# Transposed projections of two mixers as 512-column products with values and rests side by side, and their halves added on the way out of PSUM

## What is computed

```python
# first mixer
q, k, v = jnp.split(x @ w_qkv, 3, axis=-1)
...
# second mixer
u = h @ w_in
cuts = [CONV_WIDTH, 2 * CONV_WIDTH, 3 * CONV_WIDTH, 3 * CONV_WIDTH + LRU_WIDTH]
a_b, a_c, a_x, r_gate, r_x = jnp.split(u, cuts, axis=-1)
y_a = a_b * causal_depthwise_conv(a_c * a_x, conv_a_w)
xr = causal_depthwise_conv(r_x, conv_b_w) + conv_b_b
y_b = jax.nn.gelu(r_gate) * rg_lru(xr, rg_a_w, rg_a_b, rg_x_w, rg_x_b, rg_lambda)
y = jnp.concatenate([y_a, y_b], axis=-1) @ w_out
```

## Time and profile before

| | |
|---|---|
| median of 3 executions | 890.99 us |
| the profiled execution's own time | 891.4 us |
| its span | 889.3 us |
| instructions | 13261 |
| TensorE busy (matmul) | 880.2 us, 99% |
| VectorE busy | 694.1 us, 78% |
| ScalarE busy | 501.6 us, 56% |
| GpSimd busy | 29.0 us, 3% |

### The profile page before, as it was taken

One profiled execution on the slowest core, in us unless ns is written; L12 is line 12 of the kernel. 1 busy time (PEld: TensorE's weight loads), 2 busy tenths in 40 slices (PEclk: granted clock), 3 DMA queues, 4 the chain that ended last, 5 costly groups with the idle time before them and its releaser, 6 DMA issues.

```text
span 889.3 us, 13261 instructions
## 1 busy us (share of the span) xinstructions
PE 880.2 (99%) x4833; PEld 747.9 (84%) x4833; DVE 694.1 (78%) x735; ACT 501.6 (56%) x673; POOL 29.0 (3%) x52
## 2 busy tenths in 40 slices
...
DMA packets 117091, 208.04 MB, mean 234 GB/s; under 512 B 7236, under 2 KB 81068, under 8 KB 111928
## 3 DMA queue, kind: packets, MB, share of 16 engines
...
...
q0 software_dynamic: 192, 0.05, 0.0%
...
## 4 chain that ended last, share of the span: by engine, by line
PE 93%; DVE 4%; DMA 2%; issue 1%; ACT 1%; SPq 0%; DVEq 0%; ACTq 0%
PE ub L1937 11%; PE tp L1937 10%; PE acc L1837 7%; PE acc L1838 7%; PE acc L1840 7%; PE ub L1939 5%; PE acc L1800 5%; PE tp L1939 5%; PE acc L1802 5%; PE acc L1801 5%; PE tp L1957 4%; PE acc L1957 3%; PE acc L1923 3%; PE acc L1925 3%; PE acc L1924 3%; PE ub L2183 1%
## 5 line engine op out<-in xcount | busy, mean ns | idle before, releaser
L1157 DVE TENSOR_TENSOR w_lo<-w_raw,w_hi 128x1024 fp32r<-128x1024 f32 x283 | 341.8, 1222 | 105.1 <-ACT w_hi L728 104.7
L728 ACT ACTIVATE w_hi<-w_raw 128x1024 fp32r<-128x1024 f32 x283 | 296.8, 1057 | 211.9 <-PE acc L1840 49.8
L1937 PE MATMUL tp<-aT,w_hi 128*128 128x512 f32 x432 | 135.9, 396 | 0.0
L1937 PE MATMUL ub<-aT,w_hi 128*128 128x512 f32 x432 | 135.4, 395 | 0.0
L1837 PE MATMUL acc<-w_hi,hT_hi 128*128 128x512 f32 x284 | 110.8, 390 | 0.8 <-DVE w_lo L1157 0.8
L1838 PE MATMUL acc<-w_lo,hT_hi 128*128 128x512 f32 x284 | 110.6, 389 | 0.0
L1840 PE MATMUL acc<-w_hi,hT_lo 128*128 128x512 f32 x272 | 105.8, 389 | 0.0
L1939 PEld LDWEIGHTS tp<-aT,w_lo 128*128 128x128 f32 x432 | 81.2, 188 | 19.2
L1939 PEld LDWEIGHTS ub<-aT,w_lo 128*128 128x128 f32 x432 | 81.1, 188 | 18.9
L1939 PE MATMUL tp<-aT,w_lo 128*128 128x256 f32 x432 | 84.9, 278 | 0.0
L1939 PE MATMUL ub<-aT,w_lo 128*128 128x256 f32 x432 | 84.9, 278 | 0.0
...
## 6 DMA issues: line engine op xcount, KB each, us to landing
...
```

What stands on the lines that cost most here:

```text
L728: act.activation(rounded_part(v), w_raw[:, v % SLOTS, :], ACT.Copy).then_inc(hi_done, 1)
L1157: dve.tensor_tensor(rest_part(v), w_raw[:, v % SLOTS, :], rounded_part(v).bitcast(F32), ALU.subtract).then_inc(lo_done, 1)
L1937: pe.matmul(banks[f], rounded_part(v)[:, c[f]], aT[:, :, b, :], start=b == 0, stop=False)
```

## The change

U2 to U7 of the first mixer and U2 to U9 of the second become wide units. A unit now fills a pair of banks by itself: columns 0 to 255 of each bank get rounded weight by rounded values and weight's rest by rounded values, columns 256 to 511 rounded weight by the activation's rests. New steps F n get unit n out: ScalarE copies the second halves to SBUF (`rest_half`, semaphore `t_rest`), VectorE adds the first halves (`sum_halves`, semaphore `t_sum`). Units take turns on two pairs of banks (`wide_banks`), so a unit waits for the sum of the unit two before it; U8 of the second mixer has `ub`, U9 `tp`. The gelu of E1 is then done in SBUF. W1 moves from after H10 to after H8. The old step F0 of VectorE is now called N0. Cut to its core, the diff:

```diff
-ATT_STEPS = steps("""L1 U0 H2 L2 U1 H3 E0 L3 U2 H4 T0 L4 U3 H5 L5 E1 X0 G0 G1 U4 H6 L6 Y0 U5 H7 E2 S0 L7 G2 G3 G4 U6 H8 A0 S1 L8
-    U7 H9 E3 L9 W0 A1 S2 U8 H10 W1 G5 L10 A2 S3 G6 U9 H11 E4 W2 L11 A3 S4 G7 U10 H12 W3 G8 L12 A4 S5 G9
+ATT_STEPS = steps("""L1 U0 H2 L2 U1 H3 E0 L3 U2 H4 T0 L4 F2 U3 H5 L5 F3 X0 G0 G1 U4 H6 L6 Y0 F4 U5 H7 F5 S0 L7 G2 G3 G4 U6 H8 A0 S1 L8
+    F6 U7 H9 F7 L9 W0 A1 S2 U8 H10 W1 G5 L10 A2 S3 G6 U9 H11 E4 W2 L11 A3 S4 G7 U10 H12 W3 G8 L12 A4 S5 G9
...
-LRU_STEPS = steps("""B6 U0 H2 L2 U1 H3 E0 L3 M6 U2 H4 T0 L4 C0 B7 U3 H5 E1 L5 U4 H6 G0 L6 M7 X0 U5 H7 S0 F0 X1 G1 D0 E2
-    L7 U6 S1 H8 L8 D1 U7 H9 L9 Q0 E3 P0 U8 H10 W1 Y0 L10 R0 J0 U9 H11 E4 L11 K0 U10 H12 Z0 L12 Z1
+LRU_STEPS = steps("""B6 U0 H2 L2 U1 H3 E0 L3 M6 U2 H4 T0 L4 C0 F2 B7 U3 H5 L5 F3 E1 U4 H6 G0 L6 M7 X0 F4 U5 H7 S0 N0 X1 G1 D0 F5
+    L7 U6 S1 H8 W1 L8 D1 F6 U7 H9 L9 Q0 F7 P0 U8 H10 Y0 L10 R0 J0 F8 U9 H11 L11 F9 K0 U10 H12 Z0 L12 Z1
     U11 H13 L13 I0 U12 H14 U13""")
 
...
+        def wide_banks(n):
+
+            if n < 8:
+                return acc[:, 2:4, :] if n % 2 == 0 else acc[:, 0:2, :]
+            return ub[:, :, :] if n == 8 else tp[:, :, :]
 
...
-        C0 = {"qkv1": 0, "win": 4, "qkv2": 5}
+        C0 = {"qkv1": 0, "win": 1, "qkv2": 2}
+        W0 = {"qkv1": 0, "win": 6}
...
-            def copy_features(u, bank, dst, b):
-
-                act.wait_ge(w_used, parts_to(u + 2))
-                act.activation(dst[:, b:b + 3:2, :], bank.rearrange("p (b n) -> p b n", n=TOK), ACT.Copy).then_inc(cT_a, 1)
+            def rest_half(u, n, dst, chunks):
+
+                act.wait_ge(w_used, parts_to(u + n + 1))
+                b, banks = 4 * chunks[n // 2] + 2 * (n % 2), wide_banks(n)
+                act.activation(dst[:, b:b + 2, :], banks[:, :, TOK:], ACT.Copy).then_inc(t_rest, 1)
 
...
-                elif step == "E" and n < 4:
-                    copy_features(U_QKV1 + 2 * n, acc[:, 2 * (n % 2), :], qkT, 4 * QKV_CHUNKS[n])
+                elif step == "F":
+                    rest_half(U_QKV1, n, qkT, QKV_CHUNKS)
...
-                    act.wait_ge(w_used, parts_to(U_WIN + 4))
-                    b = 4 * WIN_CHUNKS[n]
-                    act.activation(uT[:, b:b + 4, :].rearrange("p (b a) n -> p b a n", a=2), blocks_of(acc[:, 2:4, :]),
-                                   ACT.Gelu_apprx_tanh).then_inc(lru_gelu, 1)
+                    act.wait_ge(t_sum, W0["win"] + 2)
+                    gate = uT[:, 4 * WIN_CHUNKS[n]:4 * WIN_CHUNKS[n] + 4, :]
+                    act.activation(gate, gate, ACT.Gelu_apprx_tanh).then_inc(lru_gelu, 1)
                     act.preload_act_table_set("sigmoid_and_others")
...
-                elif step == "E":
-                    act.wait_ge(w_used, parts_to(U_WIN + 2 * n + 2))
-                    b = 4 * WIN_CHUNKS[n]
-                    banks = ub[:, :, :] if n == 4 else acc[:, 2 * (n % 2):2 * (n % 2) + 2, :]
-                    act.activation(uT[:, b:b + 4, :].rearrange("p (b a) n -> p b a n", a=2), blocks_of(banks),
-                                   ACT.Copy).then_inc(lru_u, 1)
+                elif step == "F":
+                    rest_half(U_WIN, n, uT, WIN_CHUNKS)
...
-            def copy_features(u, bank, dst, b):
-
-                dve.wait_ge(w_used, parts_to(u + 2))
-                dve.tensor_copy(dst[:, b + 1:b + 4:2, :], bank.rearrange("p (b n) -> p b n", n=TOK)).then_inc(cT_v, 1)
+            def sum_halves(base, n, dst, chunks):
+
+                b, banks = 4 * chunks[n // 2] + 2 * (n % 2), wide_banks(n)
+                part = dst[:, b:b + 2, :]
+                dve.wait_ge(t_rest, base + n - 1)
+                dve.tensor_tensor(part, part, banks[:, :, 0:TOK], ALU.add).then_inc(t_sum, 1)
 
...
-                elif step == "E" and n < 4:
-                    copy_features(U_QKV1 + 2 * n, acc[:, 2 * (n % 2) + 1, :], qkT, 4 * QKV_CHUNKS[n])
+                elif step == "F":
+                    sum_halves(W0["qkv1"], n, qkT, QKV_CHUNKS)
...
-                    dve.wait_ge(lru_u, 2)
+                    dve.wait_ge(t_sum, W0["win"] + 6)
                     dve.tensor_tensor(uT[:, 4:8, :], uT[:, 4:8, :], uT[:, 8:12, :], ALU.mult).then_inc(lru_p, 1)
...
-            def project_T(u, h, banks, i=None, per=0):
-
-                for q in range(2):
-                    v = 2 * u + q
-                    part_ready(v, i, per)
-                    for f in range(2):
-                        outp = banks[f][:, h * TOK:(h + 1) * TOK]
-                        for k in range(4):
-                            c, b = slice(k * HALF + f * P, k * HALF + (f + 1) * P), 4 * q + k
-                            wh, wl = rounded_part(v)[:, c], rest_part(v)[:, c]
-                            pe.matmul(outp, wh, aT_hi[:, b, :], start=b == 0, stop=False)
-                            pe.matmul(outp, wh, aT_lo[:, b, :], start=False, stop=False)
-                            last = pe.matmul(outp, wl, aT_hi[:, b, :], start=False, stop=b == KB - 1)
-                    last.then_inc(w_used, 1)
-
...
-                    c = n // 2
-                    if c >= 2 and n % 2 == 0:
-                        pe.wait_ge(cT_a, C0["qkv1"] + c - 1)
-                        pe.wait_ge(cT_v, C0["qkv1"] + c - 1)
-                    if 1 <= c < 4:
-                        project_T(U_QKV1 + n, n % 2, [acc[:, 2 * (c % 2) + p, :] for p in range(2)])
+                    if n >= 4 and (n < 8 or n % 2 == 0):
+                        pe.wait_ge(t_sum, W0["qkv1"] + (n - 3 if n < 8 else n // 2 + 1))
+                    if n < 8:
+                        project_T_wide(U_QKV1 + n, [wide_banks(n)[:, f, :] for f in range(2)])
                     else:
-                        project(U_QKV1 + n, n % 2, lambda t: acc[:, 2 * (c % 2) + t, :])
+                        project(U_QKV1 + n, n % 2, lambda t: acc[:, (2, 0)[n // 2 - 4] + t, :])
                 elif step == "U" and n >= 12:
...
-                    c = n // 2
                     if n == 2:
                         pe.wait_ge(ada_out, 8)
-                    if c == 2:
+                    if 4 <= n < 8:
+                        pe.wait_ge(t_sum, W0["win"] + n - 3)
+                    if n == 8:
+                        pe.wait_ge(lru_i, 1)
+                    if n == 9:
                         pe.wait_ge(cT_a, C0["win"] + 1)
                         pe.wait_ge(cT_v, C0["win"] + 1)
-                    if c == 3:
-                        pe.wait_ge(lru_gelu, 1)
-                    if c == 4:
-                        pe.wait_ge(lru_i, 1)
-                    project_T(U_WIN + n, n % 2, ub_banks if c == 4 else [acc[:, 2 * (c % 2) + p, :] for p in range(2)])
+                        pe.wait_ge(ada_out, 12)
+                    project_T_wide(U_WIN + n, [wide_banks(n)[:, f, :] for f in range(2)])
                 elif step == "U" and n >= 10:
                     if n == 10:
-                        pe.wait_ge(lru_u, 2)
+                        pe.wait_ge(t_sum, W0["win"] + 6)
                     if n in (10, 12):
                         pe.wait_ge(y_hi, n // 2 - 4)
```

More of the change, by code:

```diff
@@ L343, in block_program @@
         x_ready = sem("x_ready")
+        t_rest = sem("t_rest")
+        t_sum = sem("t_sum")
         chunk_a = sem("chunk_a")
@@ L680, in _ @@
                                    pattern=[[-1, n]], channel_multiplier=1).then_inc(consts, 1)
-            for step, n in ATT_STEPS:
-                if step == "E" and n < 3:
-                    start_sums(0, n)
+            for third in range(3):
+                start_sums(0, third)
             pool.wait_ge(o_ready, HEADS)
@@ L806, in copy_T, with copy_v @@
                                ACT.Copy, scale=scale).then_inc(cT_a, 1)
-            def copy_v(u, n):
+            def copy_v(u, n, bank):
                 act.wait_ge(w_used, parts_to(u + 2))
-                act.activation(vtok[:, 0, n * CH:(n + 1) * CH], acc[:, 2 * n, :], ACT.Copy).then_inc(v_a, 1)
+                act.activation(vtok[:, 0, n * CH:(n + 1) * CH], acc[:, bank, :], ACT.Copy).then_inc(v_a, 1)
             act.dma_start(gain[0:1, 0, :], gains[0].rearrange("(a n) -> a n", a=1)).then_inc(gain_loaded[0], 16)
@@ L848, in _ @@
                     copy_chunk(U_QKV1, acc[:, 0, :], T0["qkv1"])
-                elif step == "E" and n < 4:
-                    copy_features(U_QKV1 + 2 * n, acc[:, 2 * (n % 2), :], qkT, 4 * QKV_CHUNKS[n])
+                elif step == "F":
+                    rest_half(U_QKV1, n, qkT, QKV_CHUNKS)
                 elif step == "E":
-                    copy_v(U_QKV1 + 2 * n, n - 4)
+                    copy_v(U_QKV1 + 2 * n, n - 4, (2, 0)[n - 4])
                 elif step == "T":
@@ L1110, in _ @@
                 elif step == "E":
-                    copy_v(U_QKV2 + 2 * n, n - 4)
+                    copy_v(U_QKV2 + 2 * n, n - 4, 2 * (n - 4))
                 elif step == "B":
@@ L1414, in copy_T, with copy_v @@
                                   scale, None, ALU.mult).then_inc(cT_v, 1)
```

(10 more changed lines are left out.)

8 lines of the change are left out of this document (4 added, 4 removed).

## The result

The changed kernel takes **899.99 us** (median of 5 executions) against 890.90 for the kernel before on the same chip. One of the five took 1466 us with TensorE's clock at 0.56 of full speed all through; without it the median is 899.76 us and the ratio 1.0094, 95% interval 1.0082 to 1.0107. The predicted time was 897.6 us, the range 894.0 to 901.0.

What follows compares the result with a forecast made beforehand. TensorE's instruction stream was taken as the span, busy 880.2 of 889.3 us. Second mixer +6.1 and first mixer +0.5 give +6.6 on the profiled 891.4, 898.0; less 0.4 for the median, 897.6 us, range 894.0 to 901.0.

Steps and rivals of the forecast that it cites:

- E1: Second mixer, the gelu step on ScalarE, queued before H6: the prediction named no wait and no cost for it.
- The gain per unit: Both mixers: each wide unit saves TensorE 0.20 us, 14 units -2.8 us if nothing waits.
- The hole: Second mixer, before U4: TensorE stands still 4.9 us for sum F2, queued on VectorE behind convolution C0.
- The chain behind it: Second mixer, ScalarE and VectorE steps from H8 to L10 and L12: U10 starts 4.95 us late, U12 5.9.
- The clock: Rival, chance 0.20: TensorE's clock falls to half in the idle 4.9 us before U4, costing 2.5 us; 900.1 us.
- The norm: End of the second mixer: VectorE runs without a gap into the norm, TensorE has 0.3 us slack; +6.1 us.
- Weights come by freed slots and move with TensorE: Weight loads: DMA issue order on SP and POOL is untouched, and loads shift with TensorE; no separate cost given.
- The first mixer: Waits for sums F4 at U6 and F6 at U8, about 0.9 each: gain 1.2, waits 1.7, +0.5 us.
- No wait at all: Rival, chance 0.05: F2 lands before U3 ends and all 14 units give 0.20 us each; 888.2 us.
- only the hole: Rival, chance 0.17: ScalarE and VectorE catch up by U10, leaving U9's 3.3 us and +0.5; 894.4 us.
- wide products give nothing: Rival, chance 0.03: wide units save no time, so only the waits are left; about 899 us.

Runs made afterwards that it cites:

- The last run: Changed kernel with U8, U9 narrow, W1 behind R0, F2 ahead of C0, F4 and F6 earlier, gelu behind H10, J0 behind H11: 891.87 us, ratio 1.0007.
- the filler: Changed kernel plus 19 unused 512-column products on TensorE just before U4 of the second mixer: 898.23 us, ratio 1.0081 to the kernel before.
- the profile shown: Changed kernel measured again without any edit, for a profile at the full clock: 899.74 us, ratio 1.0094 to the kernel before.
- undoing the hole alone: Changed kernel with only the sum F2 moved ahead of the convolution C0 in the second mixer: 898.38 us, ratio 1.0085 to the kernel before.

## Why the prediction was right, and where its terms were off

**The gain per unit.** 0.20 us was right (a wide unit takes 5.57 us, from 318.90 to T0's first product at 324.47). But it was credited to the stages, and no version's time fell by it. The text had read that TensorE never waits inside the two stages, and drew from it that work taken away is worth its full length. The last run speaks against that: 1.2 us less work in its second mixer, and the stage ends where it did. In the forecast this did no harm, for the gain was spent in the hole anyway.

**The hole** was put at 4.9 us and is 4.6 (4.55 in the row). **The chain behind it** came out as in the working: with the clock held by the filler, H8 is 3.87 late (predicted 3.9), the square root 4.67 (4.6), L10 5.40 (5.26), U10 4.97 (4.95) and L12 6.46 (6.45). F7, the moved W1 and F6, F8, F9 are all in that sum. That U10 fits to 0.02 is in part luck: L10 was put 0.14 too early, and the step from L10 to U10 took off 0.3 us of room where the text itself speaks of 0.5 and the run shows 0.43.

**The clock** was a rival at 0.20, priced 2.5 us; it came true, at 1.5 us by the medians and 1.7 at U10. Predicted time and measurement, 897.6 against 899.99, differ mostly by this; with the clock held the filler's run took 898.23, still 0.6 above. The price could have been read closer: the nearer bound given was 1.6 us, eight products at half speed. The reading that a hole of that length might do it rested on the 3.1 us wait at the start and had no row of its own. The Trainium skill's page "TensorE: Matmul & The Clock Gate", section "What's actually happening", ties the clock to how busy the array has been, and the two runs agree: the same kernel with the hole filled by 19 products kept 1.00.

**The norm.** Forecast 6.1 at the norm; measured 7.95 with the clock's fall and 6.89 with the clock held. The 0.8 us above the forecast lie behind L12: the 0.3 us of room that the text took off are not there, and 0.43 more are lost between L12 and the SwiGLU, where ScalarE waits 3.29 us for the weight load that L12 releases. In other runs up to 1.4 us went that way (the last two columns of the table). In the changed kernel itself ScalarE waits for TensorE there:

```profile
393.47 1.06 ACT L735 ACTIVATE w_hi<-w_raw 128x1024 fp32r<-128x1024 f32 x1 [2.31 <-PE acc L2036]
```

"Weights come by freed slots and move with TensorE" missed this: SyncE's load waits for `lo_done`, which VectorE's L steps count, so it moves with VectorE.

**The first mixer** was put at +0.5, with waits of 0.9 at U6 and U8. Over five profiles it is +0.1 to +1.3, 0.6 in the mean, with 0.3 to 1.5 at U6; the profile shown is the one with the least wait there. Sign and size hold.

**What the prediction did not see** is the second sum behind C0. Its schedule had F3 done at 337.4 and U5 not before 341.9, and so called it in time; that E1 and H6 wait for F3 as well was not looked at. TensorE shows no wait for it in the changed kernel, but it is why undoing the hole alone gained 1.4 us instead of some 7.

"No wait at all", "only the hole" and "wide products give nothing" are out: the hole stands in two profiles, U10 waits 1.5 us on top of it, and the wide unit's 5.57 us is in the rows. The sum of "only the hole" is wrong in itself: 3.3 + 0.5 on the profiled 891.4 is 895.2, less 0.4 makes 894.8, and the text took the 0.4 off twice. The range's lower end should have been 0.4 higher; the measured time is far from it.
